# Moving one block of 128 tokens from scattered gates to one-hot gates, and starting the row gathers during the search

## What is computed

```
q = (xt @ wq).reshape(TOKEN_BLOCK, PEER_HEADS, 2, half)         # 8 heads
s1, s2 = scores against key1, key2                              # 128 keys each
v1, i1 = lax.top_k(s1, 16);  v2, i2 = lax.top_k(s2, 16)
sc, pos = lax.top_k(v1[..., :, None] + v2[..., None, :], 16)    # of 256 pairs
experts = e1 * 128 + e2                                         # 16 of 16384 experts
gate = softmax(sc)
act  = gelu(einsum('thkd,td->thk', u[experts], xt)) * gate
out  = einsum('thk,thkd->td', act, v[experts])
```

## Time and profile before

| | us |
|---|---|
| median of 3 runs | 4469.14 (4467.87 to 4476.68) |
| the profiled execution's own time | 4451.02 |
| its span in the trace | 4449.4 |
| PE busy in the span | 4185.1 |
| DVE busy | 3044.1 |
| POOL busy | 1466.3 |

### The profile page before, as it was taken

One profiled execution on the slowest core, in us unless ns is written; L12 is line 12 of the kernel. 1 busy time (PEld: TensorE's weight loads), 2 busy tenths in 40 slices (PEclk: granted clock), 3 DMA queues, 4 the chain that ended last, 5 costly groups with the idle time before them and its releaser, 6 DMA issues.

```text
span 4449.4 us, 63937 instructions
## 1 busy us (share of the span) xinstructions
PE 4185.1 (94%) x22555; PEld 3563.2 (80%) x22555; DVE 3044.1 (68%) x6114; ACT 1557.6 (35%) x2721; POOL 1466.3 (33%) x1221
## 2 busy tenths in 40 slices
PE   7999999999899889989999998898798999999998
PEld 4668877777688768779999988888797888888886
DVE  7531037777467744447888688885468998888888
ACT  4222226555477633232223444442121222222222
POOL 0000000000044411002888788888753222222220
PEclk9999999999999989999999999999899999999999
DMA  6646323333456465233445699999898988888885
GB/s 266 243 167 244 141 76 130 117 131 113 156 173 191 141 227 184 95 106 93 93 89 108 171 267 261 262 277 273 235 347 315 303 304 285 288 288 285 287 286 197
DMA packets 479233, 913.43 MB, mean 205 GB/s; under 512 B 188818, under 2 KB 270114, under 8 KB 475412
## 3 DMA queue, kind: packets, MB, share of 16 engines
q1 hardware_dynamic: 321524, 509.44, 35.2%
q0 software_dynamic: 151136, 363.35, 27.1%
q10 hardware_dynamic: 6336, 37.75, 2.3%
HBM read 747.38 MB, written 188.17 MB: 210 GB/s over the span
## 4 chain that ended last, share of the span: by engine, by line
PE 34%; POOL 10%; DMA 5%; DVE 4%; issue 2%; ACT 0%; SPq 0%; DVEq 0%; ACTq 0%; POOLq 0%
PE ph_gate_ps L2489 15%; PE ph_hid_ps L2414 9%; PE ph_hid_ps L2489 7%; POOL scratch_scattered L2364 5%; POOL ph_ring L2370 4%; DMA ph_ring<-in_u_rows,held_tiles 4%; PE ph_hid_ps L2404 2%; DVE ph_ring L2795 1%; PE ph_score_ps L2422 1%; DVE held_tiles L2813 1%; DVE ph_u_lo L2621 0%; DMA scratch_scattered<-held_tiles 0%; DVE held_tiles L2809 0%; DVE ph_row_hot L2807 0%; DMA held_tiles<-scratch_scattered 0%
## 5 line engine op out<-in xcount | busy, mean ns | idle before, releaser
L2364 POOL DMA_INDIRECT scratch_scattered<-held_tiles x384 | 670.1, 1745 | 285.9 <-DVEq L2718 151.0
L2414 PE MATMUL ph_hid_ps<-ph_n_hi,ph_u_hi 128*128 128x384 f32 x2048 | 706.1, 345 | 50.3 <-DVE ph_u_lo L2621 50.3
L2414 PE MATMUL ph_hid_ps<-ph_n_lo,ph_u_hi 128*128 128x384 f32 x2048 | 697.3, 340 | 0.0
L2414 PE MATMUL ph_hid_ps<-ph_n_hi,ph_u_lo 128*128 128x384 f32 x2048 | 696.8, 340 | 0.0
L2390 POOL DMA_INDIRECT ph_ring<-in_v_experts,ph_pick_again x256 | 240.0, 937 | 775.5 <-DVE held_tiles L2901 743.4
L2795 DVE CUSTOM_DVE_ANT_0 ph_ring<-ph_ring,ph_n_rows 128x1024 f32<-128x1024 f32 x256 | 309.5, 1224 | 208.9 <-DMA ph_ring<-in_u_rows,held_tiles 207.9
L2414 PEld LDWEIGHTS ph_hid_ps<-ph_n_hi,ph_u_hi 128*128 128x128 f32 x2048 | 395.2, 193 | 55.9 <-DVE ph_u_lo L2621 55.7
L2414 PEld LDWEIGHTS ph_hid_ps<-ph_n_lo,ph_u_hi 128*128 128x128 f32 x2048 | 394.7, 193 | 0.2
L2414 PEld LDWEIGHTS ph_hid_ps<-ph_n_hi,ph_u_lo 128*128 128x128 f32 x2048 | 394.0, 192 | 0.0
L2370 POOL DMA_INDIRECT ph_ring<-in_u_rows,held_tiles x256 | 331.3, 1294 | 142.8 <-DVE held_tiles L2795 85.5
L2901 DVE SCALAR_TENSOR_TENSOR held_tiles<-ph_ring,ph_factor,held_tiles 128x1024 f32<-128x1024 f32 x254 | 325.0, 1280 | 0.0
(11 more groups left out here) (398 smaller groups left out, 9759.7 us busy)
## 6 DMA issues: line engine op xcount, KB each, us to landing
ph_u_raw<-in_tiles SPq DMA_DIRECT2D x136, 512.0 KB
ph_v_raw<-in_v_experts SPq DMA_DIRECT2D x124, 512.0 KB, 4.8
scratch_hidden<-ph_hidden SPq DMA_DIRECT2D x128, 384.0 KB, 3.5
ph_u_raw<-scratch_hidden SPq DMA_DIRECT2D x124, 384.0 KB, 5.0
proj_w_ch<-in_w_ch SPq DMA_DIRECT2D x49, 512.0 KB, 3.7
mb_w_raw<-in_w_branch POOLq DMA_DIRECT2D x48, 512.0 KB, 3.9
scratch_gate_tiles<-ph_gates SPq DMA_DIRECT2D x48, 512.0 KB, 7.9
ph_hidden<-scratch_gate_tiles SPq DMA_DIRECT2D x124, 192.0 KB, 4.0
```

The costliest lines, as they stand in the source:

```text
L2364: pool.indirect_dma_start(d["scattered"], bass.IndirectOffsetOnAxis(place_of[:, at:at + 1], 0), held[:, 2, GM + at:GM + at + 1], None, com ...
L2414: mm = pe.matmul(hid_halves[r][:, c, :], u[r][a][:, k, :], n2[b][:, k, c * CUT:(c + 1) * CUT], start=(k == 0 and a + b == 0), stop=(k == K ...
```

## The change

Blocks given to scatters go from 3 to 2 (`ST` = 2), so 512 tokens get their gates by one-hots (`GM` = 512). That makes 32 gate steps in place of 24, a tail of 16 tiles in place of 32, 32 scatters for a head in place of 48 (256 in all, 384 before), and 8 clearing DMAs in place of 12.

The gathers start with head 0: one after every fourth scatter for heads 0 to 4, then three for every two scatters for heads 5 to 7. The first 36 go to a new ring, `early_ring`, in memory that the search leaves free and that the second gates buffer takes later. DVE does one dot after each `split` from period 2 on (36 in all), one in each tile of the bridge (7), 2 + 3 in a gate step (6 before), and 4 in a tile of the tail, 2 where it also prepares weights. DVE's periods are written out one after the other, no longer as a loop. The last block's gate pieces are issued two at a time in the first four tiles of the tail.

```diff
-                CLEARS = (6, 6, 0)
+                CLEARS = (4, 4, 0)
...
-ST = 3
+ST = 2
...
+            soon.enter_context(nc.sbuf_tensor("ph_early_pad", [P, 14, D], F32))
+            early_ring = soon.enter_context(nc.sbuf_tensor("ph_early_ring", [P, NRING, D], F32))
...
-        FIRST_AT = (22, 24, 26, 28)
+        FIRST_AT = (8, 10, 12, 14)
...
+        EARLY = 36
...
+        def u_row(n):
+
+            return (early_ring if n < EARLY else ring)[:, n % NRING, :]
...
-                store_gates(BLOCKS - 1, range(PIECES))
...
+                    if y < PIECES // 2:
+                        store_gates(BLOCKS - 1, range(2 * y, 2 * y + 2))
...
+                    if n == EARLY:
+                        pool.wait_ge(hid_mm[1], PERIOD // 2 * (PH - 2) + 1)
-                    pool.indirect_dma_start(ring[:, n % NRING, :], None, d["u_rows"], bass.IndirectOffsetOnAxis(
+                    pool.indirect_dma_start(u_row(n), None, d["u_rows"], bass.IndirectOffsetOnAxis(
...
-                    if h == PH // 2:
-                        pool.wait_ge(hid_mm[1], PERIOD // 2 * (PH - 2) + 1)
                     for n in range(SCATTERS):
                         scatter(h, n)
-                        if h >= PH // 2:
+                        for _ in range((n % 4 == 3) if h < PH - 3 else 1 + n % 2):
                             gather(next(gathers))
...
+                        if s == 1 and x == 0 and r == 0:
+                            act.wait_ge(dotted, EARLY)
...
                     def split(x):
                         low((1 + x) % 2, PERIOD // 2 * h + (3 + x) // 2)
+                        if h >= 2:
+                            dots(1)
...
-                periods(dve, period)
+                for h in range(PH):
+                    period(h, h % 2, h == 0, h == PH - 1)
...
                 for x in range(BRIDGE):
                     low((1 + x) % 2, PERIOD // 2 * PH + (3 + x) // 2)
+                    dots(1)
...
-                            dots(3 if j >= 1 else 0)
+                            dots(2 if b == 1 else 3)
...
-                    dots(3 if y in FIRST_AT else 3 + (y % 4 != 0) if y < TAIL - 1 else PICKS)
+                    dots((2 if y in FIRST_AT else 4) if y < TAIL - 1 else PICKS)
```

More of the change, by code:

```diff
@@ L2095, in stage_peer_topk @@
             n2_rows = rows.enter_context(nc.sbuf_tensor("ph_n2_rows", [P, GT, D], F32))
+        with ExitStack() as soon:
+            soon.enter_context(nc.sbuf_tensor("ph_early_pad", [P, 14, D], F32))
+            early_ring = soon.enter_context(nc.sbuf_tensor("ph_early_ring", [P, NRING, D], F32))
         with ExitStack() as first:
@@ L2720, in _, with dots @@
                 SELECT, COLLECT = 5 * 2 * TT + 5 + 3 + 2 * len(PAIR_ROWS) + len(FIRST_ROWS) + 5 * TT + 5 + 2, 3 + 2 * 2 + 7
+                done = 0
+                def dots(count):
+                    nonlocal done
+                    for n in range(done, min(done + count, PICKS)):
+                        if n == 0:
+                            dve.wait_ge(rows_in, 16 * GT)
+                        dve.wait_ge(u_row_in[n % NRING], 16 * (n // NRING + 1))
+                        row = u_row(n)
+                        dve.tensor_tensor_reduce(row, row, n2_rows[:, n % GT, :], 1.0, 0.0, ALU.mult, ALU.add,
+                                                 pick_dot[:, pick_at(n):pick_at(n) + 1]).then_inc(dotted, 1)
+                    done = min(done + count, PICKS)
                 def period(h, s, first, last):
@@ L2783, in _ @@
                     dve.sem_inc(gates_mm[b], 1)
[L2785 to L2795, removed]
-                                                 pick_dot[:, pick_at(n):pick_at(n) + 1]).then_inc(dotted, 1)
-                    done = min(done + count, PICKS)
                 def step(j):
```

## The result

| | before | change |
|---|---|---|
| median, us | 4468.51 (4466.02 to 4476.68) | **4360.86** (4358.22 to 4363.70) |
| profiled execution, us | 4451.02 | 4358.22 |
| its span, us | 4449.4 | 4356.6 |

The ratio is 0.9756 with a 95% interval of 0.9739 to 0.9773: 2.4% faster. From profile to profile it is 93 us, from median to median 108 us.

The account below looks back on a forecast made before the run. POOL was taken to bound the gate steps; with search and bridge ending at 2506, 646 us of steps and a 149 us tail, turn 0 starts 56 us earlier; with 6 saved behind, 4389 profiled, 4407 us median, range 4372 to 4446.

Parts of the forecast that it names:

- POOL bounds the steps: Gate steps of the kernel before: six scatter and gather pairs at 3.69 us make the 22.1 us of a step.
- Search and bridge: Search to bridge end: rows coming late in DVE's order move the end from 2484 to 2506, +22 us.
- the lower bound: Search and bridge: DVE's own length alone, without late rows, costs 7 us at least.
- Gate steps: The 32 gate steps: PE bounds them at 20.2 us each, 646 us, between 624 and 680.
- Tail: The 16 tail tiles: uneven row supply makes 149 us, between 133 and 171.
- Behind the tail: Around turn 1, after the tail: 6 us of PE's lost time saved.
- From the profile to the median: Whole kernel: 4389 us for the profiled execution becomes 4407 us for the median.
- rival A: From the bridge on: PE-bound, rows land as wanted, tail takes 133 us; 4366 us in all, chance 0.15.
- B: Gate steps: DMA bounds them, a step takes 21.2 us and the tail 160; 4450 us, chance 0.1.
- D: Tail: tiles keep the old 10.7 us, so 175 us in place of 149; 4433 us, chance 0.18.
- C: Search: dots beside POOL's scatters hold it up; 4453 us, slower kernel once scatters reach 2.43 us; chance 0.07.

Follow-up runs that it names:

- two blocks only: The change without the early start: two scattered blocks, 32 gate steps, gathers from head 4 on as before; 4437.96 us, ratio 0.9928.
- early rows only: The change's early start of the gathers, but with three scattered blocks and 24 gate steps as before; 4459.13 us, ratio 0.9982.
- before once more: The kernel before, with no edit, timed and profiled a second time; 4462.23 us, ratio 0.9989.
- late sixth rows: The change without dots in the search's last period, with a sixth row in gate steps 27 to 31 and four fewer tail rows; 4347.26 us, ratio 0.9731.

## Why the prediction was right in direction and too high

**Why both parts are needed.** "POOL bounds the steps" was the reading, and each part alone leaves POOL the bound: two blocks only, because six rows a step still have scatters between them; early rows only, because the 384 scatters end too late. Against before in their own batch they gave 32 and 11 us, against before once more 24 and 3; together it is 108. Leaving out all the scatters, which no kernel can, gave 113. Once POOL is below PE's time a step costs what PE's own work costs, and further relief buys nothing there.

**Search and bridge, +22 forecast, +17 measured.** The place and the total were near, the course was not, and that they were near is in part luck. PE was to idle in periods 6 and 7 and the bridge, with waits for rows of `ph_early_ring` growing; in fact DVE waits for that ring 1.9 us in all, and period 6 is full. Head 4's last scatter starts at 2475.4, not at about 2492, and the 40th row is issued at 2479.6 in place of 2489. Its dot starts 8 us earlier than in the sum. But between it and the `low` for the last tile stand 4.7 us of the end of head 7 that the sum had left out, and PE takes 1.7 us longer for that tile, behind its pause. These nearly cancel, which makes 2503.8 for 2506. The early gather is cheaper than the one that I took, 1190 ns for 1338, in POOL's groups of the change from 2088 to 2500 us:

```profile
L2374 POOL DMA_INDIRECT scratch_scattered<-held_tiles x165 | 289.5, 1754 | 204.8 <-DVEq L2730 150.2 <-issue 50.2 <-DMA scratch_scattered<-held_tiles 4.3
L2382 POOL DMA_INDIRECT ph_early_ring<-in_u_rows,held_tiles x36 | 42.8, 1190 | 11.0 <-issue 11.0
```

About half of the delay was DVE's own length, which the prediction had as the lower bound (7, measured 8), and half were late rows in the bridge (9.4). I had taken one cause as containing the other.

**Gate steps, 646 forecast, 624 measured** (627.1 less 2.8 for the transposes). This is the step that failed most: "PE's own work in one is 484.6 / 24 = 20.2 us". That divides PE's busy time over a window in which PE waited and the clock was at 0.98; with the waits gone the clock is at 1.00 and a step takes 19.5. The trace of before held the right figure: where PE doesn't wait, two groups of small matmuls start at 2514.29 and 2524.03, so half a step is 9.74 us and a step 19.5. The lower bound that stood beside it, 624, was exact: two tiles at 8.32, from an undisturbed run of 816 matmuls, and 2.8 of small matmuls, for which no row was shown. The mechanism, PE bounds the steps, was right; the size of its term was not.

**Tail, 149 forecast, 143 measured.** The way was right: rows come late in it (DVE waits 34.5 us for them), ACT's waits for stores shrink when the gate pieces are spread, and it doesn't fall to PE's 133. The rate was 348 GB/s over the whole tail. The Trainium skill (DMA: Bandwidth & Descriptors, Specifications) gives about 358 GB/s as the limit of memory for one core. The 348 of the tail is close to that, but the trace doesn't bear it out as a limit, with 410 over 20 us in the earlier trace rows; whether memory held the tail is not shown.

**Behind the tail, -6 forecast, -6.8 measured.** PE's waits around turn 1 fell from 3.3 + 6.0 us to 4.5, and in the two stretches behind the start of turn 0 (40 and then 20 us) its clock was 0.99 and 0.93 where it was 0.96 and 0.83. PE's groups that waited in the change (the 1.9 us of the first stand at the end of the turns, and before has them too):

```profile
L2499 PE MATMUL ph_hid_ps<-ph_n_lo,ph_n_hi 128*128 128x512 f32 x576 | 142.6, 392 | 1.9 <-DVE held_tiles L2889 1.9
L2499 PE MATMUL ph_gate_ps<-ph_v_hi,ph_n_hi 128*128 128x512 f32 x256 | 102.5, 400 | 4.5 <-DVE ph_n_hi L2846 4.5
```

**From the profile to the median, +18 forecast, +3 measured.** The profiled execution of the change took 4358.22, its median is 4360.86. I carried the distance of one short execution of before over to a kernel that has none: 15 us. Where it comes from is open. Before once more, profiled at 4460.42, is 9.4 us longer than the first trace, with 8 more in the tail and 5 in the start of the stage, and 5 less in the steps; that is one pair of traces.

In sum, 46 us too high: 15 from the base, 22 from the steps, 6 from the tail, 5 from the search and 1 behind the tail, less 3 for a later start of the stage. The range began at 4372, just above rival A, and so left out the rival nearest to what came.

**The rivals.** A (PE-bound from the bridge on, 4366) is nearest in time and half right in mechanism: the steps were PE-bound at 19.5, but the search paid and the tail was 143. B is refuted by the change itself, whose steps take 19.5 us at a DMA share of 0.93. D didn't come: a tile of the tail takes 9.0 us, not 10.7. C, the slower one, rested on the rule that POOL and DVE contend (the Trainium skill, GPSIMD Engine Reference, Key points). In the search, where dots now run, the scatter's mean is 1754 ns, against 1743 in the earlier trace rows; so C's 2.43 us, with 0.30 of issue in it, was far off. In the steps it is 1847 against 1749, with more of DVE's work beside it; whether that is the page's contention was not separated. The equal means that the prediction held against C were no clean test: `low` and `differ` have two inputs in SBUF as the dot has, and they run in the search of before too.

**The better version.** Removing the last period's six dots gives a span of 4344.1 against 4356.6 and a median of 4346.91 against 4360.86. Its ratio, 0.9743, and that of the change, 0.9756, have overlapping intervals. Against before in their own batches the two gain 117 and 108 us, so 9 us of the 14 are left; by the timing alone they are likely, not shown, and the search shorter by 15 us in the trace is their cause if they are real. By the same measure the kernel without dots in the bridge (118) and the one with late sixth rows (119) are as good. Open is what else holds the tail above PE's 133: taking rows away brought it to 135 and 136, 8 and 11 us less, but only where the steps paid as much or more.

## What to carry to other kernels

Take the cost of an engine's own work from a stretch where it never waits, not from its busy time in a window where it does: where PE never waited it was 3% less, the largest error here. When one engine bounds through the sum of two kinds of work, cutting either may give little and cutting both much, so price the total and ask which queue waits for its last item. And look at the distance between the profiled execution and the median before carrying it over: here it was 18 us before and 3 after.

## What the runs showed of the hardware

A pause of PE can cost more than its length. In the bridge of the change PE waited 4.50 us; timeline of PE, start and length of single matmuls:

```profile
2488.97 0.34 PE L2424 MATMUL ph_hid_ps<-ph_n_hi,ph_u_lo 128*128 128x384 f32 x1
2493.81 0.45 PE L2424 MATMUL ph_hid_ps<-ph_n_hi,ph_u_hi 128*128 128x384 f32 x1 [4.50 <-DVE ph_u_lo L2633]
...
2496.94 0.52 PE L2424 MATMUL ph_hid_ps<-ph_n_lo,ph_u_hi 128*128 128x384 f32 x1
...
2498.09 0.33 PE L2424 MATMUL ph_hid_ps<-ph_n_hi,ph_u_hi 128*128 128x384 f32 x1
```

Behind it twelve matmuls start 0.28 to 0.32 us apart, then they are 0.17 apart again, as ahead of the pause: about 1.7 us on top of the 4.5. The granted clock is 0.54 from 2493.8 to 2497.3, near the lower of its two levels (1.2 and 2.4 GHz), after 1.00 from 2487.0 to 2493.8, the pause included; over the whole bridge it is 0.96.

The same instruction on POOL has more than one price. A gather takes 997 ns in the median in the search and 1407 in `ph_ring` behind it. DMA's share alone doesn't set it: in the gate steps the median is 1482 at a share of 0.93, in the tail 1014 at 0.98, and the gathers of v behind the tail take 936 at 0.87. What does was not found.
